# Between the two products of a pair: moving one sum in VectorE's program order

## What is computed

```python
def block(xt):                                   # 128 tokens
    ...                                          # scores s1, s2 by head, top 16 of each, top 16 of their sums
    gate = jax.nn.softmax(top_s, axis=-1)        # 8 heads x 16 experts for each token
    act = gelu(einsum('thkd,td->thk', u_tab[eid], xt))
    w = gate * act
    return einsum('thk,thkd->td', w, v_tab[eid])
```

## Time and profile before

| | |
|---|---|
| three runs, median | 3784.19 us (3777.92 to 3784.67) |
| profiled execution, its own time | 3773.32 us |
| its span, first to last instruction | 3771.5 us |
| mean granted TensorE clock | 0.918 |
| first gather to last gather issued | 831.7 to 3724.4 us |
| busy over the span: TensorE, VectorE, ScalarE, GpSimd | 82%, 71%, 36%, 32% |
| bytes over the span | 1281.06 MB, mean 340 GB/s |

### The profile page before, as it was taken

One profiled execution on the slowest core, in us unless ns is written; L12 is line 12 of the kernel. 1 busy time (PEld: TensorE's weight loads), 2 busy tenths in 40 slices (PEclk: granted clock), 3 DMA queues, 4 the chain that ended last, 5 costly groups with the idle time before them and its releaser, 6 DMA issues. The chain is left out here.

```text
span 3771.5 us, 31162 instructions
## 1 busy us (share of the span) xinstructions
PE 3078.5 (82%) x7880; PEld 1410.6 (37%) x7880; DVE 2671.1 (71%) x5254; ACT 1365.1 (36%) x3576; POOL 1198.4 (32%) x1092
## 2 busy tenths in 40 slices
PE   7889998988988989768988888798787677677676
PEld 4545554433433334323433333343332223223222
DVE  4356663136868778777888887877778878878884
ACT  3223332023443333344434433433453334334332
POOL 0000000013433334333544433443335444444442
PEclk9989998998999999888999999999898889889888
DMA  3321113459999999999999999999999999999996
GB/s 138 103 97 41 48 34 131 154 202 421 404 394 361 390 396 425 423 399 398 425 426 427 426 426 419 395 425 424 420 350 423 426 427 419 426 427 400 425 427 266
DMA packets 207881, 1281.06 MB, mean 340 GB/s; under 512 B 24048, under 2 KB 37616, under 8 KB 61936
## 3 DMA queue, kind: packets, MB, share of 16 engines
q0 software_dynamic: 147456, 1073.81, 68.7%
q1 hardware_dynamic: 55232, 195.61, 13.6%
q10 hardware_dynamic: 5040, 9.96, 0.7%
HBM read 1250.98 MB, written 28.31 MB: 339 GB/s over the span
## 5 line engine op out<-in xcount | busy, mean ns | idle before, releaser
L1344 PE MATMUL l_acc<-l_rows,l_diag 128*128 128x512 f32 x2624 | 1415.9, 684 | 600.3 <-ACT l_diag L1501 587.2
L1218 POOL DMA_INDIRECT l_rows<-in_peer_uv,l_at x1024 | 1177.7, 1150 | 1696.5 <-DVE l_acc L1679 846.0
L1344 PEld LDWEIGHTS l_acc<-l_rows,l_diag 128*128 128x128 f32 x2624 | 535.6, 214 | 1415.9 <-ACT l_diag L1501 857.1
L1669 DVE SCALAR_TENSOR_TENSOR l_rows<-l_rows,l_xn 128x1024 f32<-128x1024 f32 x640 | 762.9, 1223 | 142.3 <-DMA l_rows<-in_peer_uv,l_at 109.9
L1669 DVE SCALAR_TENSOR_TENSOR l_rows<-l_rows,all_xt 128x1024 f32<-128x1024 f32 x384 | 460.3, 1224 | 148.4 <-DMA l_rows<-in_peer_uv,l_at 125.0
L1493 ACT ACTIVATE l_dots<-l_dots 128x2 f32<-128x2 f32 x512 | 103.7, 203 | 1036.4 <-DVE l_rows L1669 1034.5
L1679 DVE SCALAR_TENSOR_TENSOR l_acc<-l_rows,l_wts,l_acc 128x1024 f32<-128x1024 f32 x272 | 349.5, 1285 | 98.2 <-ACT l_wts L1497 98.0
L117 PE MATMUL l_pa<-all_ring,all_xt 128*128 128x512 f32 x688 | 310.6, 603 | 4.5 <-PEq L71 4.5
L1497 ACT ACTIVATE l_wts<-l_dots,l_gates 128x1 f32<-128x1 f32 x1024 | 293.5, 287 | 16.8
L117 PE MATMUL l_pa<-l_ring,all_xt 128*128 128x512 f32 x656 | 293.8, 599 | 0.0
L1211 POOL CAST l_at<-l_expert 128x16 uint32<-128x16 f32 x64 | 20.5, 320 | 831.0 <-DVE l_expert L1655 830.8
(11 more groups left out here) (262 smaller groups left out, 2893.1 us busy)
## 6 DMA issues: line engine op xcount, KB each, us to landing
l_ring<-in_w_late SPq DMA_DIRECT2D x54, 1024.0 KB, 9.0
all_ring<-in_w_late SPq DMA_DIRECT2D x54, 1024.0 KB, 8.8
l_rows<-in_peer_uv,l_at POOLq DMA_INDIRECT x1024, 17.3
kept_s<-l_yt ACTq DMA_DIRECT2D x32, 256.0 KB, 7.7
l_s_in<-kept_s SPq DMA_DIRECT2D x64, 128.0 KB, 7.0
mix_w_branches<-in_w_branches_kept SPq DMA_DIRECT2D x8, 768.0 KB, 4.8
k_x<-in_x SPq DMA_DIRECT2D x8, 512.0 KB, 6.0
k_w<-in_w_keys SPq DMA_DIRECT2D x2, 2048.0 KB, 10.7
```

The source lines that it names most:

```text
L1218: pool.indirect_dma_start(out=rows[:, r % SLOTS, :], out_offset=None, in_=A["peer_uv"], in_offset=bass.IndirectOffsetOnAxis(ap=at[:, c % 2 ...
L1344: ins = pe.matmul(acc2[:, hs], diag[n_pe(r) % DIAGS][:], rows[:, r % SLOTS, D + half * HB:D + (half + 1) * HB], start=first, stop=last)
L1669: dve.scalar_tensor_tensor(out=u, in0=u, scalar=1.0, in1=xn_of(t), op0=ALU.mult, op1=ALU.mult, accum_out=dots[:, n:n + 1]).then_inc(dot_do ...
```

## The change

In a slot with a pair of its own, VectorE runs the sum of the preceding pair between the two products, in place of behind both. No instruction is added or removed, and no semaphore, buffer or DMA changes. A second VectorE row of a pair would stand behind both products as before, but no pair has one. Where the preceding pair has no VectorE row, and in the first slot, the order is the same as before.

```diff
                     if job.kind in programs:
                         programs[job.kind](job)
+                g = pair_of(s - 1)
+                sums = [r for r in (2 * g, 2 * g + 1) if not on_tensor(r)] if g is not None else []
                 if pair_of(s) is not None:
                     dot(2 * pair_of(s))
+                for r in sums[:1]:
+                    weigh(r)
+                if pair_of(s) is not None:
                     dot(2 * pair_of(s) + 1)
-                g = pair_of(s - 1)
-                if g is not None:
-                    for r in (2 * g, 2 * g + 1):
-                        if not on_tensor(r):
-                            weigh(r)
+                for r in sums[1:]:
+                    weigh(r)
                 if g is not None and (2 * g + 2) % NSEL == 0:
                     finish(2 * g // NSEL)
```

## The result

The changed kernel takes 3846.8 us, median of four runs (3843.78 to 3852.59), beside 3781.1 us for the kernel before, run four times beside it: ratio 1.0182, 95% interval 1.0165 to 1.0199. It is slower by about 68 us (by the ratio; the medians are 65.7 us apart). The direction was forecast, the size was not: 3798 us was expected, and 3826 us was the upper end of the range. The profiled execution has a span of 3841.9 us against 3771.5.

The account below looks back on a forecast made before the run. Bound by a DMA ceiling of about 426 GB/s, with dips from the VectorE, ScalarE, TensorE loop: 12.0 us for 841 to 1400 plus 1.9 for later dips, 13.9 on 3784.2, gives 3798 us; range 3781 to 3826 (8 in 10).

Parts of the forecast that it names:

- What bounds the kernel: Gather stage: ceiling of about 426 GB/s; in 841 to 1400 us a loop through VectorE, ScalarE and TensorE, never a landing.
- the cover: Stretches at 425 or 426 GB/s: the DMA queue hides both shifts, since VectorE waits 64 times for landings; nothing charged.
- the four later dips: Stretches below the ceiling after 1640 us: 8.4 us for about 7 passings less 4.6 for earlier gathers, halved to 1.9 us.
- The passings: 841 to 1400 us: ten times the path goes from second product to ScalarE and TensorE, each 1.20 us later, 12.0 us.
- The wait for the weight: Second product now behind a late weight: 1.14 us once in 841 to 1400 us; table-load excess 3.1 us, high end only.
- The forecast stall of 1.46 us: After a product needing a table change, VectorE stands still ahead of the sum; only 0.26 us excess charged, high end alone.
- Rival 1: Faster: dips are GpSimd's waits for the sum, 30% shorter by earlier release; 26 us won, 3758 us; chance 0.13.
- Rival 2: No change: nearly equal paths and saturated bandwidth take back the loss; 0 to 6 us remain, 3784 to 3790; chance 0.20.
- Rival 3: Slower by more: most waits count, paths short by under 1.2 us become longest; 31 us, 3815, far end 3845; chance 0.20.
- the 1.14 us of earlier release: Sum starts one product earlier, freeing an even row's buffer sooner; credited -1.14 us at the gather ending 841 to 1400 us.
- The forecast of the marks: Changed profile: longer diagonal waits, more weight waits mostly near 1.4 us, first stretch about 386 GB/s, long saturated stretches unchanged.

Follow-up runs that it names:

- e6: Kernel before, with the sum between the products only where the preceding pair belongs to tiles 5 to 7 (96 sums): 3776.3 us, ratio 0.9999 to the kernel before.
- e7: Sum of the preceding pair ahead of both products: 3916.5 us, ratio 1.0369 to the kernel before, 70 us above the changed kernel.
- e8: Kernel before, with the sum moved behind the slot's expert search part (at the end of a tile as before): 3773.9 us, ratio 0.9991 to the kernel before.
- e14: Changed kernel, with ScalarE's weights at the head of its slot where the order allows it: 3803.7 us, ratio 1.0070 to the kernel before.
- e13: Kernel before, with ScalarE's weights ahead of its copies and sigmoids where the order allows it: 3755.7 us, ratio 0.9949 to the kernel before.
- e10: Sum between the products, but of the pair before the preceding one (a tile's last pair summed at once): 3812.6 us, ratio 1.0091 to the kernel before.
- e11: Sum behind both products, but of the pair before the preceding one (a tile's last pair summed at once): 3794.0 us, ratio 1.0045 to the kernel before.
- e9: Kernel before, with the slot's expert search part between the products and the sum behind both: 3811.0 us, ratio 1.0097 to the kernel before.
- e5: Kernel before, with the sum between the products only where the preceding pair belongs to tiles 2 to 4 (144 sums): 3823.7 us, ratio 1.0125 to the kernel before.
- e17: Kernel before, with products heading VectorE's slot and weights heading ScalarE's (except softmax-share slots), sum behind: 3725.2 us, ratio 0.9856 to the kernel before.

## Why the prediction was wrong

*What bounds the kernel.* Right for 841 to 1400 us, where the way through second product, ScalarE and TensorE was followed and no landing lay on it. Twelve microseconds were forecast for this stretch; the traces are 16 us apart near its end (the distance grew by 17.6 us from 841 us on). The direction was right for this reason and not by luck, but this stretch is a quarter of the loss.

*The failed step* is the one on the cover: "Where the rate is 425 or 426 both shifts are hidden. The cover is the DMA queue itself." I read the rate and took VectorE's time over from one window, 2830 to 3440 us with 72 us in 610. That holds there, and e6 shows it. For 1780 to 2330 us, at the same rate, I never looked. The row above gives 28.6 us in 741: in tile 2 rows lay ready nearly always, the queues were full and VectorE's loop took just as long as they did. A full queue with a consumer that hardly waits is two limits of about equal length, and in tile 2 a delay of VectorE showed at once. This stretch, put at nothing, lost 30 us; the other stretches at the ceiling, with 35 to 72 us of waits each, lost next to nothing.

*A second term was mis-sized*: the four later dips, with 1.9 us in the sum and 8.4 us as its upper bound, lost 25 us, most of it from 1640 to 1780 and from 2690 to 2830 us (11.0 and 10.3 us). The reason given to halve the term was that "each of these dips begins with full buffers, which hide part of a delay". VectorE waited for no landing in any of the four, so by the readings above there was nothing to hide a delay behind. Everything behind the first stretch together lost 54 us.

*The passings.* 10 x 1.20 us was two thirds of what the first stretch lost. Counting none at the ceiling missed the 30 us; taking a third of TensorE's waits for the dips missed most of the 25 us.

*The wait for the weight.* The forecast stall of 1.46 us came: of the 169 idle times ahead of a sum in the changed trace 42 are 1.4 us long, where before none is. VectorE's waits for its weight went from 114 to 238 us, most of it in 36 waits of over 2 us. They were charged with 1.1 us, and 3.1 us more at the high end; e14 against e13 puts them at about 20 us. The timeline above shows one of the long ones, with ScalarE behind a matmul; the prediction had 12 of them in its first stretch and charged one.

*Rival 1* (early release helps) is refuted by e7 and e8. GpSimd's long wait for the sum cost nothing in e8, where it was 13 us longer than before. *Rival 2* (the saturated bandwidth takes the delay back) describes the stretches at the ceiling in tiles 1 and 4 to 7 and nothing else. *Rival 3* (a path with little slack becomes the longest) was the nearest in kind; its 31 us were under half of what was measured, and it was worked out of the waits of the first stretch, where only a quarter of the loss was made.

*GpSimd.* That a gather runs slower beside a product was not forecast. At 0.74 us for the gather above it takes back most of the 1.14 us of earlier release, but e8 has nearly the same slow gathers without loss.

*The forecast of the marks.* TensorE's waits for the diagonal rose (89.2 to 94.5 us), VectorE's waits for weights rose (12 to 20 in number; 7 of the 20 are 1.4 us long, so not most), GpSimd's for the sum hardly fell (284.4 to 257.1), the first stretch fell to 381 GB/s where 386 was forecast. "The two long saturated stretches at 425 to 426 as before" failed in the first of the two: tiles 2 and 3 fell from 417 to 396 GB/s.

*What stays open.* How the 26 to 70 us divide between lateness and waits in each order: e10 against e11 gives 18.6 us for lateness, but with the buffers coming free a slot later in both, and e9 gives 34 us for another pattern of it. That the loss falls where VectorE has little time over is shown by e5, e6 and the two tables; that each single slot behaves so was only argued. Whether the merges held back behind a late second product have a share is open too, and no run shows why two dips of 140 us each lost as much as they did.

## What to carry to other kernels

A rate at its ceiling says that the queue is full, not that its consumer has time over. Before hiding a delay of the consumer behind transfers, read in every stretch how long it waits for landings: in this kernel that sum was the cover, and where it was missing the delay showed. In this kernel's program order, work that others wait for (the products) did best ahead of work that frees a buffer: the sum moved back within its slot cost nothing, though a whole slot later cost 0.45%; the products moved to the head of the slot gave 1.1%, and with ScalarE's weights at the head as well 1.4%, the fastest kernel of this study (e17). And the sum, which waits for another engine, did worse the more work that could run without it was put behind it: both products behind it cost 3.7%, one 1.8%, no product nothing.

## What the runs showed of the hardware that was not expected

An indirect gather that GpSimd issues while a product of VectorE is running ends 0.8 us after the product if it began between 0.05 and 0.9 us into it (all 464 such gathers of the changed kernel, all 249 of before): in the timeline above the product ends at 1864.74 + 1.22 = 1865.96 and the gather at 1865.10 + 1.68 = 1866.78. Most of those that start with neither a product nor a sum running take 0.94 us. Of the 1024 gathers of the changed kernel 404 began beside a product and took over 1.5 us (1.71 us on the mean), of before 219. Sums hold gathers back in the same way, but not those that start just as the sum does: in the trace of before 51 began within 0.06 us behind a sum's start, and all took 0.93 or 0.94 us. The next one of the same timeline began 0.11 us ahead of a sum and took 0.94 us:

```profile
1867.08 0.94 POOL L1218 DMA_INDIRECT l_rows<-in_peer_uv,l_at  x1 [0.30 <-issue]
1867.19 1.29 DVE L1679 SCALAR_TENSOR_TENSOR l_acc<-l_rows,l_wts,l_acc 128x1024 f32<-128x1024 f32 x1
```

The Trainium skill ("GPSIMD Engine Reference", Key points) says that GpSimd shares its interfaces to SBUF with VectorE and meets contention with VectorE instructions that have two SBUF inputs, as the product has. By that the trace agrees, with 1.71 us in place of 0.94 us on the mean of the 404 gathers; the gathers that begin together with a sum, which has two SBUF inputs too, were not held. That the shared interface is the cause was not tried.
